# A two-layer decode step: three plain column groups instead of four before the last projection, its parts 32 tiles and every head's retention 12 tiles earlier in program order

## The reference

```
proj = h @ w_in                      # columns: q 2048, k 2048, v 4096, gate 4096
q, k = rotate(q, pos), rotate(k, pos) / 16
scores = (q @ k^T) * decay
o      = scores @ v + (q @ s_prev) * decay_row
s_new  = decay_chunk * s_prev + k_dec^T @ v      # prompt: 4 chunks of 128; sample: one of 8 per sequence
y = (head_rms_norm(o) * silu(gate)) @ w_out
```

## Time and profile before

| | us |
|---|---|
| median of three runs | 3517.52 (3515.86 to 3519.99) |
| the profiled execution's own time | 3512.0 |
| its span, first to last instruction | 3510.2 |
| PE busy | 3355.9 (96%) |
| DVE busy | 2127.8 (61%) |
| ACT busy | 1118.8 (32%) |
| POOL busy | 200.6 (6%) |
| mean granted clock of TensorE | 0.991 |

### The profile page before, as it was taken

One profiled execution on the slowest core, in us unless ns is written; L12 is line 12 of the kernel. 1 busy time (PEld: TensorE's weight loads), 2 busy tenths in 40 slices (PEclk: granted clock), 3 DMA queues, 4 the chain that ended last, 5 costly groups with the idle time before them and its releaser, 6 DMA issues.

```text
span 3510.2 us, 65225 instructions
## 1 busy us (share of the span) xinstructions
PE 3355.9 (96%) x25284; PEld 2965.2 (84%) x25284; DVE 2127.8 (61%) x3225; ACT 1118.8 (32%) x1646; POOL 200.6 (6%) x157
## 2 busy tenths in 40 slices
PE   7998999999999999888999999999999999999998
PEld 7987888788778878678999999999999777777787
DVE  4466565656665566437666666767666345666666
ACT  4222222222222232214333333333332343322323
POOL 1000000000000000002000000000000222222200
PEclk9999999999999999999999999999999999999999
DMA  5466888788788888754523333333334565555534
GB/s 179 151 202 208 279 273 273 247 285 269 259 265 286 263 272 268 256 190 144 165 100 124 117 111 111 125 122 118 108 116 167 199 212 204 199 201 196 195 128 156
DMA packets 477798, 679.31 MB, mean 194 GB/s; under 512 B 32561, under 2 KB 283570, under 8 KB 474354
## 3 DMA queue, kind: packets, MB, share of 16 engines
q1 hardware_dynamic: 434882, 618.88, 53.5%
q10 hardware_dynamic: 42192, 55.98, 4.5%
q0 software_dynamic: 416, 0.28, 0.1%
HBM read 583.92 MB, written 89.52 MB: 192 GB/s over the span
## 4 chain that ended last, share of the span: by engine, by line
PE 85%; DVE 6%; issue 3%; DMA 2%; ACT 2%; SPq 1%; POOL 0%; DVEq 0%; ACTq 0%; POOLq 0%
PE low_banks L1270 57%; PE high_banks L1270 26%; PE high_banks L1273 3%; DVE WL L1900 2%; DMA area<-in_cache_v 1%; SPq L1158 1%; DVE area L2001 1%; ACT WH L1583 1%; DMA WR<-in_w_in_ret 0%; DVE x_rows L1927 0%; DVE area L2263 0%; DVE area L1974 0%; DVE area L2336 0%; DMA area<-in_x_prompt 0%; DVE XL L2344 0%
## 5 line engine op out<-in xcount | busy, mean ns | idle before, releaser
L1270 PE MATMUL low_banks<-XH,WH 128*128 128x288 f32 (+2 forms) x4632 | 1125.5, 310 | 38.7 <-DVE WL L1900 12.1
L1270 PE MATMUL low_banks<-XH,WL 128*128 128x288 f32 (+2 forms) x4632 | 1063.3, 297 | 0.0
L1270 PE MATMUL low_banks<-XL,WH 128*128 128x288 f32 (+2 forms) x4632 | 1060.8, 296 | 0.0
L1270 PEld LDWEIGHTS low_banks<-XH,WH 128*128 128x128 f32 x4632 | 769.2, 190 | 186.7 <-issue 153.9
L1270 PEld LDWEIGHTS low_banks<-XH,WL 128*128 128x128 f32 x4632 | 772.4, 190 | 0.0
L1270 PEld LDWEIGHTS low_banks<-XL,WH 128*128 128x128 f32 x4632 | 772.1, 190 | 0.0
L1270 PE MATMUL high_banks<-area 128*32 128x256 f32 (+8 forms) x4720 | 628.9, 466 | 30.8 <-DMA area<-in_cache_v 12.4
L1270 PEld LDWEIGHTS high_banks<-area 128*32 128x32 f32 (+2 forms) x4720 | 272.9, 139 | 246.1 <-issue 178.5
L1583 ACT ACTIVATE WH<-WR 128x1024 fp32r<-128x1024 f32 x272 | 287.4, 1056 | 543.4 <-PE low_banks L1270 451.6
L1900 DVE TENSOR_TENSOR WL<-WR,WH 128x1024 fp32r<-128x1024 f32 x272 | 348.1, 1280 | 133.0 <-ACT WH L1583 127.4
L2001 DVE STREAM_TRANSPOSE area<-area 128x512 f32<-128x512 f32 x512 | 334.5, 690 | 108.3 <-PE high_banks L1270 63.9
(11 more groups left out here) (184 smaller groups left out, 3256.9 us busy)
## 6 DMA issues: line engine op xcount, KB each, us to landing
area<-in_cache_k SPq DMA_DIRECT2D x512, 256.0 KB, 4.9
area<-in_cache_v SPq DMA_DIRECT2D x512, 256.0 KB, 5.3
area<-in_w_in_ret SPq DMA_DIRECT2D x162, 512.0 KB, 5.7
WR<-in_w_in_attn SPq DMA_DIRECT2D x136, 512.0 KB, 5.3
WR<-in_w_out_ret SPq DMA_DIRECT2D x66, 512.0 KB, 3.8
area<-in_state_ret SPq DMA_DIRECT2D x64, 512.0 KB, 7.5
out<-area SPq DMA_DIRECT2D x64, 512.0 KB, 5.5
WR<-in_w_in_ret SPq DMA_DIRECT2D x38, 512.0 KB, 3.7
```

The costliest lines, as they stand in the source:

```text
L1270: return nc.tensor.matmul(out, a, b, start=start, stop=stop, skip_group_check=True)
```

## The change

Four things move. (1) `FILL` goes from 128 to 96: column step 2 of head 7 becomes a group of seven products ahead of the last segment, `plan_last` keeps steps 3, 4 and 5, and all parts of the last projection come 32 tiles earlier. The list of product groups now ends with step 0, step 2 and step 1 of head 7 and has 41 groups instead of 40, so the bank sets, the quarter buffers and the weight slots swap their parity; the first product now uses bank 3, and PE waits ahead of it for both projection drains instead of one. (2) `BASE` goes from 16 to 4: every retention stage stands 12 tiles earlier, which also moves it by half a chunk against the weight splits, since 12 = 8 + 4. (3) The first head's state loads stand two tiles apart, its head load and rope keep tiles 3 and 4, and its `split_g` has the other heads' place (t = 74). (4) One `turn_v` set goes into the products with its group, the other is placed at tiles 35, 37 and 39.

```diff
--- before.py
+++ after.py
@@ -483,9 +483,9 @@
 PRODUCTS = ("a11", "s2", "s1", "s3", "a12", "s4", "a22")
 X_OF = (0, "t2", "t1", "t3", 1, 2, "t4")
 BANK_OF = (0, 1, 2, 1, 0, 2, 1)
-FILL = 128
+FILL = 96
 PER_HEAD = 64
-BASE = 16
+BASE = 4
 
 
 class Products:
@@ -527,11 +527,11 @@
     def product(self, m):
         n, i = divmod(m, 7)
         freed = {0: (n - 2, 4), 1: (n - 2, 6), 2: (n - 2, 5), 3: (n, 1), 4: (n, 0), 5: (n, 3), 6: (n, 3)}[i]
-        self.mm[m] = Stage("product", i=i, bank=3 * (n % 2) + BANK_OF[i], slot=m % 3, ready=self.splits[m],
+        self.mm[m] = Stage("product", i=i, bank=3 * (1 - n % 2) + BANK_OF[i], slot=m % 3, ready=self.splits[m],
                            freed=self.drains.get(freed), mixed=self.mixes.get(X_OF[i]), opening=m if m < 2 else None)
         out = [self.mm[m]]
         if i != 2:
-            self.drains[n, i] = Stage("product_drain", i=i, o=n % 2, bank=3 * (n % 2) + BANK_OF[i], other=3 * (n % 2) + 2)
+            self.drains[n, i] = Stage("product_drain", i=i, o=n % 2, bank=3 * (1 - n % 2) + BANK_OF[i], other=3 * (1 - n % 2) + 2)
             out.append(self.drains[n, i])
         if n and self.pairs[n - 1][2] is not None:
             h, hh = self.pairs[n - 1][2]
@@ -582,11 +582,11 @@
         put(-17, loads["v"])
         put(-14, Stage("load_head"))
     else:
-        put(-13, Stage("load_head"))
+        put(-1, Stage("load_head"))
     for k in range(8):
-        put((-12, 4)[k // 4] + 3 * (k % 4) if h else -12 + 3 * k, Stage("load_state", b=2 * (k % 4) + k // 4))
+        put((-12, 4)[k // 4] + 3 * (k % 4) if h else 2 * k, Stage("load_state", b=2 * (k % 4) + k // 4))
     for which in range(2):
-        put(-13 + which, Stage("rope", which=which, early=h == 0))
+        put((-13 if h else -1) + which, Stage("rope", which=which, early=h == 0))
     loads["g"].a["split"] = splits.get(h - 1)
     put(32, loads["g"])
     put(44, Stage("silu_g"))
@@ -613,7 +613,7 @@
         put(58 + 3 * t, Stage("gate", t=t, norm=norms[t]))
     for k in range(CH):
         splits[h] = Stage("split_g", part=h % 2, k=k, freed=freed)
-        put((74 if h else 91) + 4 * k, splits[h])
+        put(74 + 4 * k, splits[h])
     for s in at.values():
         for x in s:
             x.a["g"] = h
@@ -633,8 +633,7 @@
     at = merge(at, {last + 2: [Stage("relay_loads")]},
                {last + 4 + 6 * i: [x] for i, x in enumerate(norm_loads(2))},
                norm_last(last))
-    for hh in range(2):
-        at = merge(at, turn_values(proj.stores, HEADS - 1, hh, hh, [32 * hh + t for t in (35, 37, 39, 42)]))
+    at = merge(at, turn_values(proj.stores, HEADS - 1, 1, 1, (35, 37, 39, 42)))
     out = []
     for t in range(end + 16):
         if t == 4:
@@ -795,8 +794,8 @@
 
 
 def plan_last():
-    proj = Projections(shift=1)
-    for s in range(2, 6):
+    proj = Projections(shift=0)
+    for s in range(3, 6):
         proj.step("in1", column(HEADS - 1, s), list(range(0, KT, CH)), list(range(KT)), kind="in1", hh=s % 2, row=None if s in (2, 3) else mixed_row(HEADS - 1, s))
     for part in range(HEADS):
         order = [(s, None) for s in range(8)]
@@ -824,7 +823,7 @@
             Segment([Stage("relay_area"), Stage("load_tables")])]
     attention, begun = attention_pairs(att, proj)
     segs += [*attention, Segment(attention_tail(att, proj, begun), first=pairs)]
-    todo = [(h, s) for h in range(HEADS) for s in range(6)][4:-4]
+    todo = [(h, s) for h in range(HEADS) for s in range(6)][4:-5] + [(HEADS - 1, 2), (HEADS - 1, 1)]
     prods = Products([(column(h, s), mixed_row(h, s), (h, s - 2) if s in (2, 3) else None) for h, s in todo], {})
     segs.append(Segment(norm_between(proj, prods)))
     last = plan_last()
@@ -836,7 +835,7 @@
     opening = {9: [Stage("load_rope")], 7: begun[0], 6: begun[1], 4: [first["q"], first["k"], first["v"]], 2: begun[2]}
     inputs = layer_one_inputs(prods, opening)
     at = inputs.index(prods.mm[prods.count - 1])
-    inputs[at:at] = [Stage("split_w", slot=1, spare=0)]
+    inputs[at:at] = [Stage("split_w", slot=0, spare=0)]
     inputs += [Stage("pads")]
     segs += [Segment(inputs), Segment(layer_one(last, stored))]
     stages = [s for seg in segs for s in seg.stages]
@@ -958,7 +957,7 @@
         mix_hi = {i: mixes[:, 4 + n, :, :] for n, i in enumerate((1, 2, 3, 4))}
         used[0] = 18432
         quads, first_sum = lay("quads", [128, 2 * KT, 256]), lay("first_sum", [128, 8, 128])
-        quads = [quads[:, r * KT:(r + 1) * KT, :] for r in range(2)]
+        quads = [quads[:, r * KT:(r + 1) * KT, :] for r in (1, 0)]
         assert used[0] == 27648
         spare_chunk = [a.rearrange("p (c n) -> p c n", c=CH) for a in (first_sum.rearrange("p k n -> p (k n)"), area[:, 11520:12544])]
         staged = lay("staged", [128, 4, T])
@@ -1292,7 +1291,7 @@
             def product(g, i, bank_, slot, ready, freed, mixed, opening):
                 pe.wait_ge(sem["w_lo"], c.after(ready, "w_lo"))
                 if opening is not None:
-                    for n in (("proj0_drained", "x_lo", "drained4", "drained5"), ("proj1_drained",))[opening]:
+                    for n in (("proj0_drained", "proj1_drained", "x_lo", "drained4", "drained5"), ())[opening]:
                         pe.wait_ge(sem[n], c.before(n))
                 if freed is not None:
                     for n in adds(freed):
```

## The result

The changed kernel takes 3524.34 us (median of 10 runs, 3519.08 to 3528.63); ten runs of the kernel before beside them have a median of 3516.18 (3510.56 to 3519.99). The ratio is 1.0022 with a 95% interval of 1.0013 to 1.0032: 8.2 us slower, where +10.9 and 3528 were forecast. The profiled execution took 3525.48 us, its span is 3523.7, the mean granted clock 0.990.

The account below looks back on a forecast made before the run. PE carries 85% of the chain, so only matmuls removed or PE waits count. Terms -3.4 + 2.1 + 1.2 + 10.9 - 4.3 + 0.95 + 3.4 give +10.9 us, 3528 us as the median of the runs; range 3514 to 3539.

Parts of the forecast that it names:

- The state update behind the sample's output: Heads 1 to 7: `rs_state` starts 1.55 us later behind a weight split's copy and subtraction, idle 1.8 not 0.24; +10.9 us.
- The sign that was named for it: The period of a middle head, gate to gate, should grow by 0.8 us (1.55 less 0.75).
- The evacuation wait: Heads 2 to 6: gate and one evacuation now precede the weight subtraction that POOL slows, leaving 0.1 a head; -4.3 us.
- The group, the transposes and the first product: Plain group out, seven products in: -3.4 us; its value transposes: +2.1; first product waiting for an evacuation: +1.2.
- Head 0: Last segment's first head: -6.8 us goes with the old `turn_v`, +7.75 comes from `rs_keys`, state loads, `rs_state`, `turn_v`; net +0.95.
- The state loads: Head 0: the last two of eight loads stand behind small pad DMAs and hold PE at `rs_out`; 1.5 us, bounds 0 and 3.5.
- The clock: Two of the seven new 1.8 us idles drop the granted clock, 1.7 us each; +3.4 us, bounds 0 and 11.9.
- at the other end of the products nothing changes: Start of the last segment: its first split still waits for the same third load; 0 us.
- That every idle drops the clock: Rival: all seven new idles in front of `rs_state` drop the clock, 8.5 us more; +19.4, 3537 us; chance 0.12.
- That none does: Rival: no idle of 1.8 us drops the clock, nor do head 0's transposes; +5.8, 3523 us; chance 0.22.
- That the loss is given back at the gate: Rival: the 1.34 us gate wait vanishes in all 8 heads, -10.7, so not slower; 3515 to 3518 us; chance 0.12.
- That state loads hold longer: Rival: head 0's state loads hold PE the full 3.5 us and cost the clock, +3.7 on the forecast; 3532 us; chance 0.09.

Follow-up runs that it names:

- Both BASE runs: The kernel before with BASE 12 instead of 16: ratio 1.0034; the changed kernel with BASE 8 instead of 4: ratio 0.9998, both against the kernel before.
- the late split: Changed kernel with each chunk's weight split but the first one tile later in the last segment, behind tile 3 instead of 2: 1.0022 against the kernel before.
- the run with that edit alone: Kernel before, its first product waiting for the evacuations of both column halves of the last plain tiles: 3523.53 us in one run.
- BASE 12: The kernel before with BASE 12 instead of 16, head 0's loads and rope kept at their tiles: 3527.1 us, ratio 1.0034 against the kernel before.
- the two load orders: Changed kernel, last segment's third weight chunk loaded one product earlier: 1.0031; the same, also ahead of head 0's values: 1.0021, both against the kernel before.
- the earlier `turn_v`: Changed kernel, head 0's second `turn_v` transposes at tile 36 instead of 37, one run: segment start to head 1's first gate 165.2 us against 168.4.

## Why the prediction was right

The forecast was +10.9; side by side the medians gave +8.2 and the profiles +9.2 once the unlike start is left out. The largest term and its cause were right. That the sum came as near is in part luck: head 0 and the clock came out 2.2 and 1.7 too dear, and the start of the segment, 2.3, was not in it at all.

**The state update behind the sample's output** carried it: +10.9 forecast, +11.0 measured, with the idle of 1.8 read off three durations, the copy, the subtraction, and what stood beside them. Both BASE runs show that the phase makes it, and the late split shows that it is the order on ACT and DVE within the phase. The sign that was named for it, a middle head's period 0.8 longer, came out at 0.5.

**The evacuation wait** came out at -4.6 against -4.3. The subtraction still meets POOL (1.98), as that reading had allowed; it had been moved to where its result isn't wanted.

**The group, the transposes and the first product**: -0.1 against -0.1. The wait of 1.2 was 1.14, by the run with that edit alone.

**Head 0** was mis-sized, -1.3 instead of +0.95. `turn_v` was right (2.98 for 2.8, and its clock drop). The state loads held nothing: the forecast took 1.5, between bounds of 0 and 3.5. `rs_keys` did not wait behind the slow start, and waited 2.0 instead of 0.65 when the segment started on time at full clock. `rs_state` of head 0 waited 0.8 for 1.1.

**The clock**: +1.7 instead of +3.4.

**What the working missed**: "at the other end of the products nothing changes". The same load waits for the same things, but it landed 5.4 us after its issue instead of 4.1, and the idle of 4.73 was followed by a longer stretch at half rate. It is no noise of one landing: the idle is 3.49, 3.62 and 3.77 in the three profiles with the old order of groups, and 4.64 to 5.22 in the eight of the changed kernel and its variants where the load isn't put ahead of the values. What stands there in the changed kernel alone is a store of the values of column step 2, now the second to last group:

```profile
2707.04 0.37 ACTq L1729 DMA_DIRECT2D retention_values<-area  x1
2707.44 0.54 ACTq L1730 DMA_DIRECT2D retention_values<-area  x1
2708.41 0.91 SPq L1202 DMA_DIRECT2D area<-retention_inputs  x2
```

These 576 KB are issued 1.4 us ahead of head 0's loads; in the kernel before the last store is issued 9.1 us ahead of them (2668.40 and 2677.49). The loads behind it land later from their issue, the values' second 8.8 instead of 7.7 us. No run takes the store away, so that it is the reason is likely but not shown. That this idle is worth 4 us was not in the forecast either, since I asked only what changes.

**The rivals.** That every idle drops the clock fell with one drop in seven. That none does came close (3523, and the time is 3524.3), but one did, and the transposes of head 0 dropped it too: its number was near since head 0 was better. That the loss is given back at the gate fell: the eight gate idles are 1.34 before and after, released by PE's own `rs_state`, and they move only when that distance does. That state loads hold longer fell, with no wait at 2748.91.

## What to carry to other kernels

When a block of work is moved against another with a fixed period, take the shift modulo that period first, and list for each engine which periodic job now stands in front of a latency-bound one; here 4 tiles of phase cost 11 us in front of one stage, while the removed group, with what took its place, was worth 0.1. A gain that is planned next to a full engine should be tried at each phase: BASE 4, 7 and 8 of the same change gave 1.0022, 0.9969 and 0.9998. A wait that is taken out of PE's stream can hand itself to the next instruction in the in-order stream of the engine that was waited for, so its followers have to be read before it is priced as a gain.

## What the runs showed of the hardware that I had not expected

The granted clock is not settled by an idle's length and place alone. The idle of 1.7 to 1.8 us in front of `rs_state` stands in five profiles (the changed kernel, BASE 12, the two load orders, the earlier `turn_v`), 34 times in all with the same work around it. Three were followed by 3.4 us at half rate, 31 by the full clock; and one of 1.19 us in the BASE 12 run, which is shorter, was followed by a drop, 2.1 us after it had ended. The Trainium skill ("TensorE: Matmul & The Clock Gate", HAM oscillation — how this bites in real kernels) takes gaps of this size for harmless; 31 of 34 agree, three don't. The longer idle of 2.96 to 2.98 before head 0's `turn_v` went with half rate in all four profiles that have it.

A load's landing can be a matter of its place in the queue alone: the same 512 KB took 4.6, 5.4 and 8.5 us from issue to landing, and when it was issued 3.1 us earlier behind the same values' load it landed 3.1 us later from its issue.
